# Phase 2a of a decoder trunk: the second half of each chunk's gating, split in two and emitted around the next chunk's projections

## The reference, cut to what matters

```python
gu = jax.nn.gelu(gu)
gv = layer_norm(jax.nn.gelu(gv), gm_ln_g, gm_ln_b)
# chunk_gmlp: per chunk of 128 positions and group g of 256 channels
vc = v.reshape(B, nc, L, GM_GROUPS, GM_CG)
ws = jnp.tril(gm_ws[:, :L, :L])
bias = gm_bs[:, :L].T[None, None, :, :, None]
mixed = jnp.einsum('gts,bnsgc->bntgc', ws, vc) + bias
return u * mixed.reshape(B, T, GM_WIDTH)
```

## Time and profile before

| | us |
|---|---|
| median of 3 runs | 2532.34 |
| the 3 runs | 2520.76, 2532.34, 2617.86 |
| the profiled execution, device time | 2533.17 |
| its span on the slowest core (core 4) | 2531.6 |
| spans of the 8 cores | 2438.9 to 2531.6 |
| TensorE busy, core 4 | 1753.5 (69%) |
| VectorE busy | 817.8 (32%) |
| ScalarE busy | 717.1 (28%) |
| GpSimd busy | 185.8 (7%) |

### The profile page before, as it was taken

The page is one execution under the profiler, slowest core; times in us unless marked ns, Lnnn a source line. Parts: engine busy times, 40 slices in busy tenths (PEclk is TensorE's granted clock), DMA queues, the critical chain, the costliest instruction groups (busy, mean ns, idle before and its releaser), DMA issues.

```text
span 2531.6 us, 26128 instructions; the slowest of 8 cores (2438.9 to 2531.6 us)
## 1 busy us (share of the span) xinstructions
PE 1753.5 (69%) x8168; PEld 774.9 (31%) x8168; DVE 817.8 (32%) x1520; ACT 717.1 (28%) x1292; POOL 185.8 (7%) x248
## 2 busy tenths in 40 slices
PE   1676667677455497866999528877555489759994
PEld 0222223222122143433454213333222134324441
DVE  1444434544222211231323425444322112222223
ACT  2443444444222110131111135555322111221101
POOL 1101000000000100001000010110000100010000
PEclk9987868878567698988999759999867699879997
DMA  6646456434700334227442173440410641356431
GB/s 132 144 142 152 121 158 150 147 111 131 151 2 0 54 56 67 38 62 109 68 69 39 53 160 55 84 84 30 78 18 1 89 65 21 76 99 100 67 42 67
DMA packets 164392, 208.51 MB, mean 82 GB/s; under 512 B 9952, under 2 KB 120928, under 8 KB 164256
## 3 DMA queue, kind: packets, MB, share of 16 engines
q0 software_dynamic: 102976, 93.33, 26.6%
q1 hardware_dynamic: 42848, 79.95, 10.9%
q10 hardware_dynamic: 18432, 33.56, 3.7%
HBM read 253.86 MB, written 46.27 MB: 119 GB/s over the span
## 4 chain that ended last, share of the span: by engine, by line
PE 48%; DMA 18%; DVE 13%; issue 9%; ACT 7%; POOL 3%; DVEq 1%; ACTq 1%; SPq 1%; POOLq 0%
PE PS L419 20%; PE PS L801 7%; PE PS L813 6%; PE PS L797 6%; DMA W<-w_in 6%; DMA cst<-cs 3%; DMA rss<-T 3%; PE PS L749 3%; ACT T L387 2%; DVE qks L486 2%; POOL stat L381 2%; DVE rtc L484 2%; DMA W<-w_ffn_in 1%; DMA W<-w_o 1%; DVE T L563 1%
## 5 line engine op out<-in xcount | busy, mean ns | idle before, releaser
L419 PE MATMUL PS<-W,RA 128*128 128x512 bf16 x2720 | 701.2, 417 | 82.0 <-DMA W<-w_in 80.7
L419 PEld LDWEIGHTS PS<-W,RA 128*128 128x128 bf16 x2720 | 287.4, 107 | 470.5 <-issue 213.8
L797 PE MATMUL PS<-RA,W 128*128 128x512 bf16 (+1 forms) x880 | 184.2, 353 | 19.2 <-DMA W<-w_ffn_in 19.2
L801 PE MATMUL PS<-RA,W 128*128 128x512 bf16 (+1 forms) x880 | 183.1, 351 | 7.5 <-DMA W<-w_ffn_in 7.5
L805 ACT ACTIVATE T<-PS 128x512 f32<-128x512 f32 (+1 forms) x110 | 58.7, 533 | 387.2 <-PE PS L797 347.4
L813 PE MATMUL PS<-W,RC 128*128 128x512 bf16 x748 | 162.4, 379 | 0.0
L807 DVE TENSOR_TENSOR RC<-PS,T 128x512 bf16<-128x512 f32 (+1 forms) x110 | 67.2, 612 | 294.5 <-PE PS L801 232.8
L381 POOL TENSOR_TENSOR stat<-stat,mhalf 128x1 f32<-128x1 f32 x119 | 65.3, 549 | 1210.8 <-DVE stat L378 1210.8
L561 PE MATMUL PS<-vbs,ksel 16*128 16x512 bf16 x128 | 62.2, 504 | 124.5 <-DVE S L534 66.6
L419 PE MATMUL PS<-W,RB 128*128 128x512 bf16 x544 | 127.4, 388 | 11.7 <-DMA W<-w_ret_o 11.7
L378 DVE TENSOR_SCALAR stat<-stat 128x1 f32<-128x1 f32 x119 | 18.3, 154 | 297.7 <-ACT T L508 191.9
(11 more groups left out here) (110 smaller groups left out, 1817.9 us busy)
## 6 DMA issues: line engine op xcount, KB each, us to landing
W<-w_in POOLq DMA_DIRECT2D x32, 1024.0 KB, 20.7
T<-st_in SPq DMA_DIRECT2D x128, 256.0 KB, 4.0
rss<-T ACTq DMA_DIRECT2D x128, 256.0 KB, 3.0
W<-w_ffn_in POOLq DMA_DIRECT2D x20, 1024.0 KB, 14.3
T<-xp SPq DMA_DIRECT2D x32, 512.0 KB, 3.6
cst<-cs SPq DMA_DIRECT2D x68, 128.0 KB, 3.6
W<-w_in POOLq DMA_DIRECT2D x16, 512.0 KB, 8.0
W<-w_ret_o POOLq DMA_DIRECT2D x8, 1024.0 KB, 25.2
```

The costliest lines, as they stand in the source:

```text
L419: op("pe", lambda e, kc=kc: e.matmul(PS[bank][:, 0:ncol], lhs_R[:, kc0 + kc, li * 128:(li + 1) * 128], W[slot][:, kc, coff:coff + ncol], s ...
L797: op("pe", lambda e, kc=kc, bg=bg, sg_=sg_, co=co, t0=t0, tn=tn: e.matmul(PS[bg][:, 0:tn], W[sg_][:, kc, co:co + 128], RA[:, kc, t0:t0 + t ...
L801: op("pe", lambda e, kc=kc, bu=bu, su_=su_, co=co, t0=t0, tn=tn: e.matmul(PS[bu][:, 0:tn], W[su_][:, kc, co:co + 128], RA[:, kc, t0:t0 + t ...
```

## The change

The body of P2a's loop is split into three functions. `p2a_X` holds everything up to the normalised `gv`; `p2a_Ymm` the four matmuls with `wsT` and the four steps of line 684 (for the sample chunk its VectorE work); `p2a_Ytr` the transposes and the copy to `RC`. The text now emits `X(0)`, and then for each chunk n: `Ymm(n)`, `X(n+1)`, `Ytr(n)`. The tiles for Gelu of `gu` and for the normalised `gv` are taken in turn from two: `T2[0]` and the space of `qks[0]`, `T2[1]` and the space of `qks[1]` (P1's tiles, idle in P2a). The unused values of Square go to the space of `T4[1]`, so `T2[2]` is free for the gated product of the chunk before.

```diff
-        for li in lis:
+        ggu_b = [T2[0][:], qks[0][:].rearrange("p a b -> p (a b)").bitcast(BF16)]
+        ggu_k = [("T2", 0), ("qks", 0)]
+        vn_b = [T2[1][:], qks[1][:].rearrange("p a b -> p (a b)").bitcast(BF16)]
+        vn_k = [("T2", 1), ("qks", 1)]
+        junk41 = T4[1][:].bitcast(BF16)[:, 0:D]
+
+        def p2a_X(li, q):
...
-            op("act", lambda e: e.activation(out=T2[2][:], in_=T4[0][:], func=AF.Square, accum_out=stat[:, 6:7]),
-               reads=[("T4", 0), ("stat", 4)], writes=[("T2", 2), ("stat", 4)])
+            op("act", lambda e: e.activation(out=junk41, in_=T4[0][:], func=AF.Square, accum_out=stat[:, 6:7]),
+               reads=[("T4", 0), ("stat", 4)], writes=[("T4", 1), ("stat", 4)])
...
+                op("dve", lambda e: e.scalar_tensor_tensor(out=vn_t, in0=T4[1][:], scalar=stat[:, 9:10], in1=GB[:], op0=ALU.mult, op1=ALU.add),
+                   reads=[("T4", 1), ("stat", 9), ("G", 1)], writes=[vn_key])
...
+        def p2a_Ymm(li, q):
+            sample = (li == 8)
+            gu_t, gu_key, vn_t, vn_key = ggu_b[q], ggu_k[q], vn_b[q], vn_k[q]
+            if not sample:
+                for g in range(4):
+                    op("pe", lambda e, g=g: e.matmul(PS[4 + g // 2][:, (g % 2) * 256:(g % 2) * 256 + 256], wsT[:, g, :], vn_t[:, g * 256:(g + 1) * 256],
+                                                     start=True, stop=True), reads=["wsT", vn_key], writes=[("PS", 4 + g // 2)])
+                for g in range(4):
+                    op("dve", lambda e, g=g: e.scalar_tensor_tensor(out=T2[2][:, g * 256:(g + 1) * 256], in0=PS[4 + g // 2][:, (g % 2) * 256:(g % 2) * 256 + 256],
+                                                                    scalar=bsT[:, g:g + 1], in1=gu_t[:, g * 256:(g + 1) * 256], op0=ALU.add, op1=ALU.mult),
+                       reads=[("PS", 4 + g // 2), "bsT", gu_key], writes=[("T2", 2)])
...
+        def p2a_Ytr(li):
             for kc in range(8):
                 op("pe", lambda e, kc=kc: e.transpose(TR[:, kc, :], T2[2][:, kc * 128:(kc + 1) * 128], ident[:]), reads=[("T2", 2), "ident"], writes=[("PS", 6)])
-            op("act", lambda e, li=li: e.copy(out=RC[:, :, li * 128:(li + 1) * 128], in_=TR[:, :, :]), reads=[("PS", 6)], writes=[("RC", li)])
+            op("act", lambda e: e.copy(out=RC[:, :, li * 128:(li + 1) * 128], in_=TR[:, :, :]), reads=[("PS", 6)], writes=[("RC", li)])
+
+        p2a_X(lis[0], 0)
+        for n_, li in enumerate(lis):
+            p2a_Ymm(li, n_ % 2)
+            if n_ + 1 < len(lis):
+                p2a_X(lis[n_ + 1], (n_ + 1) % 2)
+            p2a_Ytr(li)
```

More of the change, by code:

```diff
@@ L655, in build_program @@
             for j in range(2):
-                op("act", lambda e, j=j: e.activation(out=T2[0][:, j * 512:(j + 1) * 512], in_=PS[j][:], func=AF.Gelu_apprx_tanh),
-                   reads=[("PS", j)], writes=[("T2", 0)])
+                op("act", lambda e, j=j: e.activation(out=gu_t[:, j * 512:(j + 1) * 512], in_=PS[j][:], func=AF.Gelu_apprx_tanh),
+                   reads=[("PS", j)], writes=[gu_key])
             op("dve", lambda e: e.memset(stat[:, 4:8], 0.0), writes=[("stat", 4)])
@@ L690, in build_program @@
                 fw.dma("sp", gmv[:, :], T4[0][0:NS, :], ds_gmv, reads=[("T4", 0)])
+        def p2a_Ymm(li, q):
+            sample = (li == 8)
+            gu_t, gu_key, vn_t, vn_key = ggu_b[q], ggu_k[q], vn_b[q], vn_k[q]
+            if not sample:
[6 more added lines that the diff above has]
+                       reads=[("PS", 4 + g // 2), "bsT", gu_key], writes=[("T2", 2)])
+            else:
                 for g in range(4):
@@ L694, in build_program @@
                        reads=[("T4", 0), "wsb", "bsb"], writes=[("T4", 1)])
-                op("dve", lambda e: e.tensor_tensor(out=T2[2][:], in0=T4[1][:], in1=T2[0][:], op=ALU.mult),
-                   reads=[("T4", 1), ("T2", 0)], writes=[("T2", 2)])
+                op("dve", lambda e: e.tensor_tensor(out=T2[2][:], in0=T4[1][:], in1=gu_t, op=ALU.mult),
+                   reads=[("T4", 1), gu_key], writes=[("T2", 2)])
+        def p2a_Ytr(li):
             for kc in range(8):
                 op("pe", lambda e, kc=kc: e.transpose(TR[:, kc, :], T2[2][:, kc * 128:(kc + 1) * 128], ident[:]), reads=[("T2", 2), "ident"], writes=[("PS", 6)])
-            op("act", lambda e, li=li: e.copy(out=RC[:, :, li * 128:(li + 1) * 128], in_=TR[:, :, :]), reads=[("PS", 6)], writes=[("RC", li)])
+            op("act", lambda e: e.copy(out=RC[:, :, li * 128:(li + 1) * 128], in_=TR[:, :, :]), reads=[("PS", 6)], writes=[("RC", li)])
[5 more added lines that the diff above has]
+            p2a_Ytr(li)
         if gi == 0:
```

## The result

The changed kernel takes 2475.24 us (median of 10 runs) where the kernel before takes 2525.6 us (median of 10). The ratio is 0.981, with a 95% interval of 0.9783 to 0.9837: 48 us faster, 41 to 55 us by the interval. The forecast was a gain of 44 us, to 2489 us; the time lies in its range. Whether the gain passes 2% can't be told, as the interval holds 0.98. Executions that one die of the chip spent at a lower clock are left out of all ratios, and where too few others are left, only the stage is compared.

What follows compares the result with a forecast made beforehand. P2a was taken as a closed loop in which TensorE waits on VectorE and nothing overlaps. Removing 15 x 3.26 = 48.9 us, less 4.5 us for the clock, gave 44.4 us and 2489 us, range 2466 to 2513.

Steps and rivals of the forecast that it cites:

- The removed leg: P2a, first `wsT` matmul to the transposes: 3.26 us leaves each of 15 turns, 48.9 us in all.
- The chain stays: P2a, projections' end to the next `wsT` matmul: the 6.48 us through the second normalisation step stays in every turn.
- Rival C: P2a: the 6.48 us chain is hidden too, 84 us beyond the clock staying up, 2366 us; chance 0.01.
- rival D: P2b's loads or the P2a chain take longer: half the gain lost gives 2511 us, all 2533; chance 0.07.
- a sign against it: P2b's waits, about 6 and 10 us, should stay the same; the forecast is wrong if they have grown.
- The clock: P2a: it falls in each gap and bursts start low; projections 9.3 us against 9.0, 4.5 us lost over 15 turns.
- rivals A and B: P2a clock: A, whole burst at 1.2 GHz, 2556 us, chance 0.03; B, clock stays up, 2450 us, chance 0.04.
- Rival B: P2a clock stays up: projections 7.1 us, `wsT` matmuls half of 0.81, 83 us gained, 2450 us; chance 0.04.
- the nearest row: P2a projections: the present range of 8.07 to 9.62 us, as TensorE works without a break after the restart; 9.3 taken.
- the bound of 10.5 us: P2a projections if the clock rises 7.8 us after the first `wsT` matmul: gain 26 us, time 2507 us.
- The scatter: Whole kernel: runs were put at about 6 us either way, on top of the forecast's bounds of 2469 to 2507 us.

## Why the prediction was right

- **The removed leg** (3.26 us in 15 turns, 48.9 us) is what was measured: the stage shrank by 48.6 us on the mean of eight cores, and the doubled steps cost 2.36 us per turn before and, on cores 6 and 7, nothing after.
- **The chain stays.** 6.47 us per turn, the idle time ahead of the `wsT` matmuls is 98.3 us in total (50.0 and 48.3 us for the two tiles in the trace's list of that line) where 95 to 100 us were named against 105.0, and a longer chain cost time. Rival C, that it is hidden too, is what the kernel with `wsT` behind the projections did, not this change.
- **Nothing given back** (rival D): the issue of P2b's loads moved with the last chunk's chain, and the stage alone accounts for the gain. On the two profiled cores the first wait of P2b did grow, from 6.08 to 7.76 us, which the prediction named as a sign against it; the means over eight cores (17.8 and 17.9 us) show that this is scatter between cores.
- **The clock** neither stayed up nor failed to rise (rivals A and B). In the changed kernel, from stretches of its trace:

```profile
734.00:735.00 1.00, 0.00 (x0) 0.00 (x0) 0.54 (x1) 0.00 (x0) 0.94 (x1) 0.97 0.00 0
735.00:736.00 1.00, 0.00 (x0) 0.00 (x0) 0.95 (x1) 0.00 (x0) 0.00 (x0) 0.50 0.00 0
```

  It fell at about 735, 5 us into the gap. Rival B's price of 1.9 + 0.4 = 2.3 us per turn proved sound where the gap was filled: 31 us in 13 turns, 2.4 us each.
- **How soon the clock rises** was left open, between two rows. The runs show it: over the turns of all eight cores the clock rises 2.6 to 6.0 us after the first `wsT` matmul in the changed kernel. In the kernel before it rises 5.5 to 9.4 us after it, which is 2.3 to 6.2 us after the transposes, 3.26 us later. So the rise follows the start of the work without a break, as the choice of the nearest row assumed, and the bound of 10.5 us, with the rise 7.8 us after the first `wsT` matmul, did not come about. Doubling the steps of line 684 in the kernel before moved the rise by those 2.36 us too: it comes 2.6 to 6.0 us after the transposes there (six cores). One stretch of the changed kernel (core 0, first `wsT` matmul at 769.97) and one of the kernel before (core 4, transposes at 730.88) in which the clock, the third number from the end, rises from 0.50 to 1.00:

```profile
775.00:776.00 1.00, 1.00 (x4) 0.39 (x3) 0.00 (x0) 0.09 (x1) 0.00 (x0) 0.55 0.00 0
```

```profile
736.00:737.00 1.00, 1.00 (x5) 0.44 (x4) 0.00 (x0) 0.00 (x0) 0.00 (x0) 0.78 0.03 8
```

  The rise is at 775.9 and at 736.4 by these shares, 5.9 and 5.6 us after those starts.
- **The term that was off** is the clock's: 9.3 us for the projections, a loss of 4.5 us. They took 9.0 us: 231.6 less 15 x 0.81 and 13 x 6.48 leaves 135.2 us, 9.01 each, as before. I had argued that they would linger at the long end of their range, and took the mean of the three longer turns of a cycle of four, though the mean of all was known to be 9.0. The rows above do show 9.3 to 9.6 us in several turns, but the short ones of 8.0 to 8.5 us came often enough to make up for it. Without that term the sum is 48.9 us, and the time 2484 us.
- **The scatter** was taken too small for a profiled execution: single runs of the changed kernel that count in its ratio went from 2468.8 to 2491.28 us. That 2% would be just missed or met was right, and it can't be told which.

## What to carry to other kernels

Software pipelining is decided on the engine that waits: write out that engine's order, and look whether the other engines' chain still stands between two of its blocks. Here the split hid the short leg (48 us) and left the long chain in place; moving the consumer one block further hid that as well and gave 134 us more, with the same tiles. And where a gap can't be closed, its price is the gap plus the low clock after it.

## What the runs showed of the hardware

- **An added wait did not cost its full length.** The projections took 9.0 us with gaps of 6.48 us, and 8.5 us with 7.87 us (longer chain). In the kernel before they went from 9.0 to 8.8 us when the second wait grew from 2.25 to 4.61 us (312.3 less 15 x 6.43 and 13 x 6.48, over 15). So 8 of 18 us, and 3 of 35 us, of an added wait were given back. That is no rule for longer waits. The clock stood at its low level at each start in all four kernels. In the changed kernel the projections climb turn by turn to 9.6 us and fall back to 8.0, while with the longer chain they settle at 8.3 to 8.4 us in more than half of the turns (8.36, 8.37 and 8.38 us in the rows above). Turns of 17.05 us keep their place and turns of 15.3 to 16.9 us do not; why was not tried.
- **Filling work in a gap cost nothing.** 24 useless matmuls per turn made the stage 31 us shorter: the clock stayed at 2.4 GHz, and the projections took 7.07 us.
- **A third clock.** In the run with the doubled VectorE steps on the changed kernel, core 1 shows this:

```profile
750.00:753.00 3.00, 3.00 (x9) 1.07 (x8) 2.41 (x6) 0.00 (x0) 0.00 (x0) 0.50 0.00 0
...
756.00:759.00 3.00, 3.00 (x13) 1.20 (x12) 0.00 (x0) 1.19 (x3) 0.00 (x0) 0.81 0.00 0
```

  The projections of that turn took 10.01 us in place of at most 9.6, at 0.81 of the full clock where otherwise 1.00 follows. Five profiled executions show this level for a time: the first one with the tiles alone, the filled gap, both with doubled VectorE steps, and the hidden chain with the longer step. The other six, the kernel before and the changed kernel among them, never show it. It is no matter of P2a: with the gap filled, core 0 stood at it for 189 us between 306 and 633 us, ahead of P2a, and not in P2a. Nor does the kernel decide: the tiles alone have it in their first run and not in their second. By the Trainium skill (TensorE: Matmul & The Clock Gate, section "Seeing it yourself"), a limit on current takes a die to 13/16 of its clock once a third core on it runs dense matmuls. The level of 0.81 agrees with that. Two things do not. With the chain hidden, core 4 worked without a break for 54 us at 1.00, and none of the eight cores shows 0.81 at any time. And in the kernel before with doubled steps, cores 2, 3, 6 and 7 stood at 0.81 for 153 to 182 us each and cores 0, 1, 4 and 5 never, so it came by pairs of cores and not by the die. What sets it off stays open.
